# Two key batches of the cache moved into the feed-forward's inner rows, and the sample group's products gathered into fewer groups

## The chip, the cores and the metric

The kernel runs on one core of a Trainium2 chip. Its time is the device time of one execution in microseconds (us); less is better. The engines are PE (TensorE), DVE (VectorE), ACT (ScalarE), POOL (GpSimd) and SP (SyncE), which here issues the DMA transfers. Each engine works through its own list of instructions in order and waits on semaphores, so an instruction that waits also holds up all behind it on that engine.

## What is computed

One inference step of a decoder layer, for 256 prompt tokens and 8 sample tokens (one new token for each of 8 sequences, with 1024 cached positions each in 8 pages of 128):

```python
def trunk_layer(x, ...):
    x = x + 0.5 * swiglu_ffn(x, ffn1_norm, ffn1_w_in, ffn1_w_out)
    h = rmsnorm(x, mix_norm)
    u, q, k, v, qm = split(h @ w_in)                  # 1024 -> 256 + 3*512 + 256
    y_pool = pool_mixer(u, state_pool)
    q, k = rotary(rmsnorm(q)), rotary(rmsnorm(k))
    y_moba = moba_attention(q, concat(k_cache[pages], k), concat(v_cache[pages], v))
    y_mem = mem_attention(rmsnorm(qm), mk, mv)
    x = x + concat(y_pool, y_moba, y_mem) @ w_out
    return x + 0.5 * swiglu_ffn(x, ffn2_norm, ffn2_w_in, ffn2_w_out)
```

Everything is float32. A product of two float32 matrices is made of three products of rounded parts (`three`): high by high, high by low, low by high.

## The kernel before, in words

**Stages.** The first feed-forward (its inner rows, then its output product, called FFN1 out here, until 215.8 us), the mix stage (projections and all attention, until about 345 us), the output projection, and the second feed-forward.

**Weights** come through a ring of four raw buffers in units of 128x1024. SP loads a unit, ACT makes its high part (`w_hi`), DVE its low part (`w_lo`), PE uses both. FFN1 out has 22 units, numbers 48 to 69, of 24 matmuls each. The last two are taken together, bank by bank (`last_two`): PE waits for both low parts ahead of the first of its 48 matmuls.

**Key pages.** The cached keys of the eight sequences come in batches k0 to k7 of eight pages. DVE turns each batch by four STREAM_TRANSPOSE instructions of two pages each ("turn pairs", G 0 to G 31, counted in `k_turned8`), and then PE makes the batch's scores (K 0 to K 7, `key_logits`, which waits for that count). There are four slots of `kv`, an `early_slot` for k4 and a `late_slot` for values. Batches k0 to k3 are loaded in FFN1 and turned in FFN1 out; k4 to k7 are loaded and turned in the mix stage, k5 to k7 as slots come free (`free_wait`).

**The order of the mix stage** is written by hand. The projection has 16 steps r, each of four blocks P(r, tt, kk) of three 128x512 matmuls on PE. The table `EXTRA[r][i]` gives the tokens that every engine goes through ahead of block i of step r (i = 4: behind the step), and `TAIL` what follows the 16 steps. Each engine picks out the tokens that concern it, so the table sets the order on each engine. The tokens used below:

- PE: S r (sample tokens' product of step r, from the raw unit: a raw buffer is not loaded anew before its S is done), K b (key scores), V b (products with cached values), T (turns of q and k), HA h, HB h, PV h (prompt attention of head pair h: scores, turn of probabilities, product with values), MG (turn of a memory-key page; MG k waits for the copy of page k-1), A 1, A 4, A 5 (sums in the sample softmax), Y.
- ACT: W (high part of a unit), ET and ES (copies out of the projection's banks for prompt and samples; ET counts `t_evac`), HE (exponentials), HT, and the copies of even memory-key pages.
- DVE: WL (low part), G (turn pairs), NR, NQ, NV, NS, NG, ND (norms and rotary parts; NR 2 waits for ET 1), OWN, A 0, A 2, A 4 (sample softmax), HM (mask and maximum), HV (scaling of probabilities, which HB waits for), and the copies of odd memory-key pages.

S, K and V write narrow column ranges (8 or 32 columns of the array for each instruction, several ranges at once). In the table of before they stand mostly one by one between P blocks.

Of the kernel before, what the change touches and what calls it, by code (L numbers as in the profile page):

```python
# [15 lines left out]
P = 128  # L16
D = 1024
KT = D // P
DFF = 2816
HT = DFF // P  # L20
NS = 8
# [36 lines left out]
EARLY_PAIRS, AWAKE, AWAKE_2 = 16, 12, 3  # L58
# [12 lines left out]
HELD = (4, 5, 6, 7)  # L71

EARLY_SLOT, LATE_SLOT = KV_SLOTS, KV_SLOTS + 1
SLOT_OF = {("k", 0): 0, ("k", 1): 1, ("k", 2): 2, ("k", 3): 3, ("k", 4): EARLY_SLOT, ("k", 5): 0, ("k", 6): 1, ("k", 7): 2,
           ("v", 0): 3, ("v", 1): 0, ("v", 2): 1, ("v", 3): 2, ("v", 4): LATE_SLOT, ("mk", 0): 3, ("v", 5): 0, ("mv", 0): 1,
           ("v", 6): 2, ("v", 7): LATE_SLOT}
# [34 lines left out]
def layer(nc, a):  # L111

    ctx = ExitStack()
    with ctx:
# [96 lines left out]
        at[0] = region  # L211
        qp = over("qp", [P, 2, 512])
        at[0] = late_end
        early_slot = place("early_slot", [P, PAGES * 512], at=at[0])
        vp = over("vp", [P, 2, 512])
        up = over("up", [P, 2, 512])
        kT = over("kT", [P, 4, NP])
        prob_pair = over("prob_pair", [P, 2, 2, NP])
        kp = over("kp", [P, 2, 512])
        probT_pair = [probT_even, over("probT_odd", [P, 2 * NP])]  # L220
        q4 = over("q4", [P, P])
        k4 = over("k4", [P, P])
        v4 = over("v4", [P, P])
        u4 = over("u4", [P, P])
        qm_cols = place("qm_cols", [P, 2, NS, 32], at=at[0])
        qT = over("qT", [P, 4, NP])
        qmT = over("qmT", [P, 2, NP])
        mkT = over("mkT", [P, 2, NP])
        pm_cols = over("pm_cols", [P, 2, P])
        ys = over("ys", [P, KT, NS])  # L230
        stats = over("stats", [P, 80])
        m_stats = over("m_stats", [P, 4])
        joined = over("joined", [P, 3, P])
        same, repeat, quarter_of = joined[:, 0, :], joined[:, 1, :], joined[:, 2, :]
        own_y = over("own_y", [P, 2, 4, 4])
        v_cols = over("v_cols", [P, P])
        marks = over("marks", [P, 8])
        half_mark, two_mark = marks[:, 4:6], marks[:, 6:8]
        sq_one = over("sq_one", [P, 1, P])
# [6 lines left out]
        rm_pos = over("rm_pos", [P, 2 * CH])  # L246

# [9 lines left out]
        kv_loaded = [[sem(f"kv_loaded{i}_{h}") for h in range(2)] for i in range(KV_SLOTS + 2)]  # L257
# [59 lines left out]
        slots = [kv[:, i, :] for i in range(KV_SLOTS)] + [early_slot[:], late_slot[:]]  # L317
# [14 lines left out]
        def free_wait(eng, kind, b):  # L332

            if kind == "k" and b == 4:
                eng.wait_ge(w_used, U_WIN)
            elif kind == "k" and b > 4:
                eng.wait_ge(k_used, b - 4)
            elif kind == "v" and b < 5:
                eng.wait_ge(k_used, (4, 6, 7, 8, 8)[b])
            else:  # L340
                eng.wait_ge(v_used, {"mk": 1, "mv": 3}[kind] if kind != "v" else {5: 2, 6: 4, 7: 5}[b])
# [52 lines left out]
        def keys_of(u, t):  # L394
# [26 lines left out]
        }  # L421
        TAIL = ([("T", 4), ("NQ", 6), ("HV", 6), ("HV", 7), ("POOL", 0), ("MG", 4), ("HB", 6), ("HT", 6), ("HB", 7), ("HT", 7), ("MG", 5), ("NV", 6), ("ND", 5),
# [25 lines left out]
        def _(sp):  # L448
# [31 lines left out]
            def load_page(kind, b, t):  # L480

                if kind == "k":
                    if b in PAIRED:
                        pages[b, t] = page_of(b, t)
                    page = pages[b, t]
                elif b in PAIRED:
                    page = ((pairs[b, t // 2] >> 8) if t % 2 else (pairs[b, t // 2] & 255)).with_bounds(min_val=0, max_val=a["cache_v"].shape[1] - 1)
                else:
                    page = pages.pop((b, t))
                done = kv_loaded[SLOT_OF[kind, b]][t // 4]  # L490
                if kind == "k":
                    sp.dma_start(slots[SLOT_OF["k", b]][:, t * 512:(t + 1) * 512],
                                 a["cache_k"][0, ds(page, 1)].rearrange("o p h d -> p (o h d)")).then_inc(done, 16)
                else:
                    sp.dma_start(value_rows(b, t), a["cache_v"][0, ds(page, 1)].rearrange("o (b k) h d -> k (o b) (h d)", b=4)).then_inc(done, 16)
# [72 lines left out]
            for k in range(HT):  # L568
                load_unit(U_OUT1, k, 0, ffn_out[0][:, k:k + 1, :])
                if k >= HT - 2 * len(HELD):  # L570
                    for t in range(4):
                        at_ = HELD[(k - HT + 2 * len(HELD)) // 2], k % 2 * 4 + t
                        pages[at_] = page_of(*at_)
                if k == LATE_KEYS - 1:
                    sp.wait_ge(w_used, U_MEM + 4)
                if LATE_KEYS <= k < LATE_KEYS + PAGES:
                    load_page("k", 3, k - LATE_KEYS)
                    if (k - LATE_KEYS) % 2:
                        pair_pages(3, k - LATE_KEYS)
# [20 lines left out]
            load_batch("k", 4)  # L600
# [4 lines left out]
            load_batch("k", 5)  # L605
            load_projection(8)
            load_batch("k", 6)
            load_projection(9)
            load_batch("k", 7)
            load_projection(10)  # L610
            load_batch("v", 0)
            load_projection(11)
            load_projection(12)
            load_batch("v", 1)
            load_projection(13)
            load_projection(14)
            load_projection(15)
            load_batch("v", 2)
# [75 lines left out]
        def _(act):  # L694
# [196 lines left out]
            for what, k in steps():  # L891
# [16 lines left out]
                elif what == "T":  # L908
                    if k == 2:
                        act.wait_ge(k_used, 5)  # L910
# [97 lines left out]
        def _(vec):  # L1008
# [20 lines left out]
            def turn_pair(g):  # L1029

                kv_wait(vec, "k", g // 4, (g % 4 // 2,))
                vec.transpose(key_pair(g), key_pair(g)).then_inc(k_turned8, 1)  # L1032
# [269 lines left out]
            vec.wait_ge(const_set, 5)  # L1302
            ffn_out_loop(0, 0, 1)
# [4 lines left out]
            for n in range(16):  # L1308
                split(U_OUT[0] + 2 + 4 + n)
                if n < EARLY_PAIRS:  # L1310
                    turn_pair(n)
# [190 lines left out]
        def _(pe):  # L1502
# [149 lines left out]
            def key_logits(b):  # L1652
# [6 lines left out]
                pe.wait_ge(k_turned8, 4 * (b + 1))  # L1659
# [340 lines left out]
```

## Time and profile before

| | before |
|---|---|
| time, median of 3 runs | 560.54 us (560.49 to 561.45) |
| profiled execution: its span | 559.2 us |
| PE busy | 551.3 us, 99% of the span |
| DVE busy | 398.9 us, 71% |
| ACT busy | 269.2 us, 48% |
| granted TensorE clock | 1.000 |

The span runs from the first to the last instruction of the profiled execution; the median lies 1.3 us above it. Busy times of engines overlap; the time is set by the engine that others wait for.

### The profile page before, as it was taken

The numbers are of one execution on the slowest core, as the hardware profiler recorded it, in microseconds if no ns is written. First come the engines' busy times: TensorE is split into PE (matmuls) and PEld (weight loads), VectorE is DVE, ScalarE is ACT, GpSimd is POOL, SyncE is SP. The second block draws the span as 40 slices with busy tenths as digits, with TensorE's granted clock in tenths as the row PEclk, the third lists the DMA queues.
The fourth block names the chain that finished last, engine by engine and source line by source line (L and its number), as shares of the span: only waits on it lengthen the run. The fifth ranks groups of instructions, "written<-read, shape, count | busy, mean of one in ns | idle before, by whom it ended". The sixth has DMA issues, their size and how long they took to land.

```text
span 559.2 us, 13391 instructions
## 1 busy us (share of the span) xinstructions
PE 551.3 (99%) x5075; PEld 513.6 (92%) x5075; DVE 398.9 (71%) x715; ACT 269.2 (48%) x425; POOL 17.7 (3%) x24
## 2 busy tenths in 40 slices
PE   8999999999999999999999999999999999999997
PEld 8999999999899998666777679999999999999997
DVE  4687888885588877889946685689777777664444
ACT  5844464444543337344535785475444344433330
POOL 1000000000000003100000000140000000000000
PEclk9999999999999999999999999999999999999999
DMA  9799999784567664899999994566756666465523
GB/s 236 208 269 324 271 315 268 234 249 149 196 216 273 205 209 160 273 338 382 351 300 371 373 337 143 163 180 197 211 168 191 182 175 194 132 220 181 187 75 79
DMA packets 137481, 128.40 MB, mean 230 GB/s; under 512 B 10937, under 2 KB 108880, under 8 KB 137432
## 3 DMA queue, kind: packets, MB, share of 16 engines
q1 hardware_dynamic: 134703, 127.24, 72.8%
q10 hardware_dynamic: 2736, 0.61, 0.5%
q8 instruction: 26, 0.43, 0.3%
q14 instruction: 16, 0.12, 0.1%
HBM read 125.12 MB, written 2.83 MB: 229 GB/s over the span
## 4 chain that ended last, share of the span: by engine, by line
PE 85%; DVE 7%; DMA 3%; ACT 2%; issue 1%; SPq 0%; DVEq 0%; ACTq 0%
PE banks L1505 25%; PE banks L1506 25%; PE banks L1507 25%; PE banks L1665 3%; PE banks L1513 2%; DVE w_lo L1021 2%; PE banks L1939 1%; PE banks L1637 1%; DMA raw<-in_ffn_w_in 1%; PE banks L1890 1%; DMA x_rows<-in_x_sample 1%; DMA page_ids<-in_page_table 1%; PE banks L1866 1%; ACT x_hi L827 1%; DVE prob_pair L1448 1%
## 5 line engine op out<-in xcount | busy, mean ns | idle before, releaser
L701 ACT ACTIVATE w_hi<-raw 128x1024 fp32r<-128x1024 f32 x158 | 166.5, 1059 | 194.9 <-PE banks L1507 160.8
L1021 DVE TENSOR_TENSOR w_lo<-raw,w_hi 128x1024 fp32r<-128x1024 f32 x158 | 193.8, 1232 | 73.9 <-ACT w_hi L701 72.7
L1505 PE MATMUL banks<-x_hi,w_hi 128*128 128x264 f32 x752 | 214.1, 285 | 0.1
L1506 PE MATMUL banks<-x_lo,w_hi 128*128 128x264 f32 x752 | 213.0, 283 | 0.0
L1507 PE MATMUL banks<-x_hi,w_lo 128*128 128x264 f32 x752 | 213.0, 283 | 0.0
L1505 PEld LDWEIGHTS banks<-x_hi,w_hi 128*128 128x128 f32 x752 | 141.6, 188 | 0.7 <-issue 0.4
L1506 PEld LDWEIGHTS banks<-x_lo,w_hi 128*128 128x128 f32 x752 | 141.7, 188 | 0.0
L1507 PEld LDWEIGHTS banks<-x_hi,w_lo 128*128 128x128 f32 x752 | 141.0, 188 | 0.0
L1505 PE MATMUL banks<-h_hi,w_hi 128*128 (+1 forms) x352 | 100.2, 285 | 0.0
L1507 PE MATMUL banks<-h_hi,w_lo 128*128 (+1 forms) x352 | 100.2, 285 | 0.0
L1506 PE MATMUL banks<-h_lo,w_hi 128*128 (+1 forms) x352 | 100.0, 284 | 0.0
L1506 PEld LDWEIGHTS banks<-h_lo,w_hi 128*128 128x128 f32 x352 | 66.5, 189 | 0.0
L1505 PEld LDWEIGHTS banks<-h_hi,w_hi 128*128 128x128 f32 x352 | 66.2, 188 | 0.3 <-ACT mem_kv L879 0.3
L1507 PEld LDWEIGHTS banks<-h_hi,w_lo 128*128 128x128 f32 x352 | 66.3, 188 | 0.0
L1065 DVE TENSOR_TENSOR h_tmp<-banks,rstd 128x264 f32<-128x264 f32 x44 | 18.9, 429 | 22.7 <-PE banks L1507 22.7
L1032 DVE STREAM_TRANSPOSE kv<-kv 128x1024 f32<-128x1024 f32 x28 | 33.9, 1228 | 0.0
L1505 PE MATMUL banks<-w_hi,x_hi 128*128 128x512 f32 x64 | 28.0, 438 | 0.3 <-ACT qp L794 0.3
L726 ACT ACTIVATE sg<-sg 128x264 f32<-128x264 f32 x44 | 18.3, 415 | 18.2 <-DVE sg L1060 18.2
L1507 PE MATMUL banks<-w_hi,x_lo 128*128 128x512 f32 x64 | 25.3, 395 | 0.0
L1506 PE MATMUL banks<-w_lo,x_hi 128*128 128x512 f32 x64 | 25.2, 394 | 0.0
L1074 DVE TENSOR_TENSOR h_lo<-h_tmp,h_hi 128x264 f32 (+1 forms) x44 | 19.1, 434 | 3.6
L1070 DVE TENSOR_TENSOR h_tmp<-sg,h_tmp 128x264 f32<-128x264 f32 x44 | 19.0, 433 | 3.3 <-ACT sg L726 2.0
(287 smaller groups left out, 501.7 us busy)
## 6 DMA issues: line engine op xcount, KB each, us to landing
raw<-in_ffn_w_in SPq DMA_DIRECT2D x86, 512.0 KB, 4.8
raw<-in_ffn_w_out SPq DMA_DIRECT2D x44, 512.0 KB, 3.4
kv<-in_cache_k SPq DMA_DIRECT2D x56, 256.0 KB, 4.8
kv<-in_cache_v SPq DMA_DIRECT2D x48, 256.0 KB, 6.3
raw<-in_w_in SPq DMA_DIRECT2D x12, 512.0 KB, 5.2
late_slot<-in_cache_v SPq DMA_DIRECT2D x16, 256.0 KB, 4.6
raw<-in_w_out SPq DMA_DIRECT2D x8, 512.0 KB, 7.5
raw<-in_mem_w_kv SPq DMA_DIRECT2D x4, 512.0 KB, 4.0
```

Of the source, the lines that this page charges most:

```text
L701: act.activation(w_hi[:, n % RING, :], raw[:, n % RING, :], ACT.Copy).then_inc(hi_ready, 1)
L726: act.activation(sg[:, s, :], sg[:, s, :], ACT.Silu).then_inc(silu_ready, 1)
L1021: vec.tensor_tensor(w_lo[:, n % RING, :], raw[:, n % RING, :], w_hi[:, n % RING, :].bitcast(F32), ALU.subtract).then_inc(lo_ready, 1)
L1032: vec.transpose(key_pair(g), key_pair(g)).then_inc(k_turned8, 1)
L1065: vec.tensor_tensor(h_tmp[:, s, :], bank[b0 + 2 * s + 1][:, 0:N], rstd[:], ALU.mult).then_inc(gu_free, 1)
L1070: vec.tensor_tensor(h_tmp[:, s, :], sg[:, s, :], h_tmp[:, s, :], ALU.mult).then_inc(hm_ready, 1)
L1074: vec.tensor_tensor(h_lo[:, ds(c, 1), :].rearrange("p a n -> p (a n)"), h_tmp[:, s, :], h_hi[:, ds(c, 1), :].rearrange("p a n -> p (a n)") ...
L1505: pe.matmul(out, lhs[0], rhs[0], start=start, stop=False)
L1506: pe.matmul(out, lhs[0], rhs[1], start=False, stop=False)
L1507: return pe.matmul(out, lhs[1], rhs[0], start=False, stop=stop)
L1513: return pe.transpose(out, in_, ident[0:k, 0:k])
L1665: mm = pe.matmul(bank[LG_BANK][32 * hp:32 * hp + 32, half * NP:(half + 1) * NP], q_cols[:, c0:c0 + 32], keys[:, 4 * hp + c], start=(b4 == ...
```

## The change

Batches k4 and k5 get two hidden slots of their own, which lie over the inner rows `h_hi` and `h_lo` of the first feed-forward. A unit of FFN1 out uses up one inner row, and as soon as enough rows are used (`w_used`), SP loads a page of each batch over them. So 24 turn pairs, G 0 to G 23, are done before and in FFN1 out, and k6 and k7 take the slots of k0 and k1 in the mix stage. Values take other slots. Small tiles get other places in memory. In the table, K 0 to K 3 stand together, S 4 to S 7 with K 4 and K 5, K 6 and K 7 with S 8 to S 11, V 0 with V 1, V 3 with S 12 to S 15, and the sample softmax and the prompt attention begin about a step earlier. The diff, cut to its core (of the table a line only):

```diff
-HELD = (4, 5, 6, 7)
+HELD = (6, 7)
+HIDDEN = (4, 5)
+LEAD_PAIRS = (0, 1, 2)
+EARLY_PAIRS = ((3,), (4,), (5, 16), (6,), (7, 20), (8, 17), (9,), (10, 21), (11,), (12, 18), (13,), (14, 22), (15,), (19,), (23,), ())
...
+        slot_bytes, half_bytes = 4 * PAGES * 512, 4 * HT * N
+        hidden_slots = [place(f"hidden_slot{i}", [P, PAGES * 512], at=region + i * half_bytes) for i in range(2)]
...
-            elif kind == "k" and b > 4:
-                eng.wait_ge(k_used, b - 4)
+            if kind == "k":
+                eng.wait_ge(k_used, b - 5)
             elif kind == "v" and b < 5:
-                eng.wait_ge(k_used, (4, 6, 7, 8, 8)[b])
+                eng.wait_ge(k_used, (3, 4, 7, 8, 8)[b])
...
             for k in range(HT):
                 load_unit(U_OUT1, k, 0, ffn_out[0][:, k:k + 1, :])
+                if k >= 6 and k % 2 == 0:
+                    t = k // 2 - 3
+                    sp.wait_ge(w_used, U_OUT1 + 2 * t + 2)
+                    for b in HIDDEN:
+                        pages[b, t] = page_of(b, t)
+                        load_page("k", b, t)
...
-            load_batch("k", 4)
+            sp.wait_ge(w_used, U_WIN)
...
-            load_batch("k", 5)
+            load_batch("k", 6)
+            load_batch("k", 7)
             load_projection(8)
-            load_batch("k", 6)
             load_projection(9)
-            load_batch("k", 7)
...
+            for g in LEAD_PAIRS:
+                turn_pair(g)
...
                 split(U_OUT[0] + 2 + 4 + n)
-                if n < EARLY_PAIRS:
-                    turn_pair(n)
+                for g in EARLY_PAIRS[n]:
+                    turn_pair(g)
...
-                pe.wait_ge(k_turned8, 4 * (b + 1))
+                pe.wait_ge(k_turned8, 4 * (b + 1) if b in HELD else 4 * HELD[0])
...
-            6: {0: [("NG", 3)], 1: [("G", 28)], 2: [("G", 29)], 3: [("WL", 9), ("G", 30)], 4: [("S", 8)]},
+            6: {0: [("NG", 3)], 1: [("G", 28)], 2: [("G", 29)], 3: [("WL", 9), ("G", 30)], 4: [("G", 31)]},
```

On DVE, in steps 3 and 4, the list of before has the turn pairs of k4 (early_slot) and of k5 (kv) on both sides of NR 2, whose first instructions are the four `rot<-qp`:

```order
L1021 TENSOR_TENSOR w_lo<-raw,w_hi 128x1024
L1032 STREAM_TRANSPOSE early_slot<-early_slot 128x1024 x4
L1032 STREAM_TRANSPOSE kv<-kv 128x1024 x2
L1164 TENSOR_TENSOR rot<-qp,rope_q 128x128 x4
L1172 TENSOR_TENSOR qp<-rot 128x16x8
L1173 TENSOR_TENSOR qp<-rot 128x16x8
L1032 STREAM_TRANSPOSE kv<-kv 128x1024 x2
L1129 TENSOR_REDUCE ss_h<-sq_h 128x16
```

The same place in the changed list:

```order
L1037 TENSOR_TENSOR w_lo<-raw,w_hi 128x1024
L1183 TENSOR_TENSOR rot<-qp,rope_q 128x128 x4
L1191 TENSOR_TENSOR qp<-rot 128x16x8
L1192 TENSOR_TENSOR qp<-rot 128x16x8
L1148 TENSOR_REDUCE ss_h<-sq_h 128x16
```

Six pairs ahead of NR 2 and two behind its rotary part have gone to FFN1 out; the other eight, of k6 and k7, stay behind NR 2.

On PE, around the first head pair's scores (HA 0, `kT,qT`), before had V 0, a P block, HA 0, S 13 and V 1 in this order, then three P blocks (nine rows like the last, left out), then HB 0:

```order
L1939 MATMUL banks<-kv,p_cols 8x128 x32
L1505 MATMUL banks<-w_hi,x_hi 128x512
L1506 MATMUL banks<-w_lo,x_hi 128x512
L1507 MATMUL banks<-w_hi,x_lo 128x512
L1866 MATMUL banks<-kT,qT 128x128 x2
L1866 MATMUL banks<-kT,qT 128x256 x2
L1637 MATMUL banks<-raw,xs 8x128 x8
L1939 MATMUL banks<-kv,p_cols 8x128 x32
L1505 MATMUL banks<-w_hi,x_hi 128x512
```

After, V 0 and V 1 stand ahead of HA 0, and behind it come three P blocks and HB 0 (`prob_pair`):

```order
L1960 MATMUL banks<-kv,p_cols 8x128 x64
L1887 MATMUL banks<-kT,qT 128x128 x2
L1887 MATMUL banks<-kT,qT 128x256 x2
L1526 MATMUL banks<-w_hi,x_hi 128x512
L1527 MATMUL banks<-w_lo,x_hi 128x512
L1528 MATMUL banks<-w_hi,x_lo 128x512
```

S 13 and V 1 no longer stand between HA 0 and HB 0; S 14 and V 3 leave the place between HA 1 and HB 2, and V 4 with a memory-key page that between HA 2 and HB 4.

On PE, at the end of step 7, the changed list has K 6 and K 7 (32 instructions) and S 8 to S 11 (32) next to each other:

```order
L1528 MATMUL banks<-w_hi,x_lo 128x512
L1686 MATMUL banks<-kv,q_cols 32x256 x32
L1658 MATMUL banks<-raw,xs 8x128 x32
L1526 MATMUL banks<-w_hi,x_hi 128x512
L1527 MATMUL banks<-w_lo,x_hi 128x512
L1528 MATMUL banks<-w_hi,x_lo 128x512
L1847 MATMUL banks<-own_by_half,joined 128x8
```

In the list of before K 7 stands a step later, behind S 10, and the six products stand at five places; from NR 2's release to K 6 the changed list has 16 P blocks, T 0 and T 1.

## Rows read from the trace of the kernel before

**Rows 1.** The page's first part: busy time, share of the span, instructions.

```profile
PE 551.3 (99%) x5075; PEld 513.6 (92%) x5075; DVE 398.9 (71%) x715; ACT 269.2 (48%) x425; POOL 17.7 (3%) x24
```

**Rows 2.** The list of waits, PE: total us, times, longest us.

```profile
PE banks L1513 <- DVE prob_pair L1448: 0.7, 1, 0.7
PE banks L1513 <- ACT kv L722: 0.6, 1, 0.6
PE banks L1505 <- ACT qp L794: 0.3, 1, 0.3
```

**Rows 3.** Timeline of DVE in FFN1 out: start, duration, instruction, idle before it.

```profile
190.75 1.22 DVE L1021 TENSOR_TENSOR w_lo<-raw,w_hi 128x1024 fp32r<-128x1024 f32 x1 [0.53 <-ACT w_hi L701]
193.69 1.23 DVE L1021 TENSOR_TENSOR w_lo<-raw,w_hi 128x1024 fp32r<-128x1024 f32 x1 [0.56 <-ACT w_hi L701]
```

**Rows 4.** Timeline of SP: loads of units 68 and 69, four page numbers read between them.

```profile
193.87 0.33 SPq L456 DMA_DIRECT2D raw<-in_ffn_w_out  x1
196.42 0.33 SPq L456 DMA_DIRECT2D raw<-in_ffn_w_out  x1
```

**Rows 5.** DMA issues of FFN out units: count, KB each, median us to landing.

```profile
raw<-in_ffn_w_out SPq DMA_DIRECT2D x44, 512.0 KB, 3.4
```

**Rows 6.** Timeline of PE around S 0 to S 3.

```profile
220.21 0.39 PE L1507 MATMUL banks<-w_hi,x_lo 128*128 128x512 f32 x1
220.53 1.93 PE L1637 MATMUL banks<-raw,xs 128*8 128x128 f32 x64
222.39 0.50 PE L1505 MATMUL banks<-w_hi,x_hi 128*128 128x512 f32 x1
222.73 0.39 PE L1506 MATMUL banks<-w_lo,x_hi 128*128 128x512 f32 x1
```

**Rows 7.** Timeline of PE: K 4 and T 0.

```profile
242.62 1.93 PE L1665 MATMUL banks<-early_slot,q_cols 128*32 128x256 f32 x32
...
246.68 0.60 PE L1513 MATMUL banks<-ident,qp 128*128 128x128 f32 x4
```

**Rows 8.** Timeline of DVE: the start of NR 2, and G 30 and G 31.

```profile
241.86 0.85 DVE L1164 TENSOR_TENSOR rot<-qp,rope_q 128x128 f32<-128x128 f32 x4
...
260.75 2.36 DVE L1032 STREAM_TRANSPOSE kv<-kv 128x1024 f32<-128x1024 f32 x2
```

**Rows 9.** Busy times from NR 2's start to the end of G 31: window, length, engines, clock, DMA share, GB/s.

```profile
241.70:263.11 21.41, 21.41 (x193) 14.25 (x192) 19.81 (x37) 8.75 (x13) 0.00 (x0) 1.00 1.02 373
```

**Rows 10.** Timeline of DVE: starts of OWN 0 and A 0, and A 4's last.

```profile
264.14 0.28 DVE L1201 TENSOR_TENSOR rot<-q,k 128x128 f32<-128x128 f32 x1
...
266.48 0.69 DVE L1375 TENSOR_REDUCE stats<-banks 128x8 f32<-128x512 f32 x1
...
278.34 0.60 DVE L1410 TENSOR_SCALAR p_own<-ones,stats 128x128 f32<-128x128 f32 x2
```

**Rows 11.** Timeline of PE: S 13, V 1, P, HB 0; then S 14 and P.

```profile
284.67 0.62 PE L1637 MATMUL banks<-raw,xs 128*8 128x128 f32 x16
285.11 1.93 PE L1939 MATMUL banks<-kv,p_cols 128*8 128x128 f32 x64
286.97 0.50 PE L1505 MATMUL banks<-w_hi,x_hi 128*128 128x512 f32 x1
...
289.16 1.15 PE L1513 MATMUL banks<-ident,prob_pair 128*128 128x128 f32 x6
...
294.47 0.62 PE L1637 MATMUL banks<-raw,xs 128*8 128x128 f32 x16
295.02 0.50 PE L1505 MATMUL banks<-w_hi,x_hi 128*128 128x512 f32 x1
```

**Rows 12.** Timeline of DVE: HV 0, two scalings.

```profile
288.50 0.55 DVE L1448 TENSOR_SCALAR prob_pair<-prob_pair,rc 128x128 f32<-128x128 f32 x2
```

**Rows 13.** Busy times of line L1706's matmuls (all alike) at the program's start.

```profile
1.00:3.80 2.80, 2.80 (x13) 2.80 (x14) 1.00 0.85 201
3.80:5.30 1.50, 1.48 (x13) 1.28 (x12) 1.00 0.63 158
```

More of the change, by code:

```diff
@@ L57 @@
 ACT_PAGES = (0, 2, 4, 6)
-EARLY_PAIRS, AWAKE, AWAKE_2 = 16, 12, 3
+AWAKE, AWAKE_2 = 12, 3
 UNITS = 12
@@ L70 @@
 PAIRED = (0, 1, 2, 3)
-HELD = (4, 5, 6, 7)
[L73 to L76, printed above, removed]
+HELD = (6, 7)
+HIDDEN = (4, 5)
+LEAD_PAIRS = (0, 1, 2)
+EARLY_PAIRS = ((3,), (4,), (5, 16), (6,), (7, 20), (8, 17), (9,), (10, 21), (11,), (12, 18), (13,), (14, 22), (15,), (19,), (23,), ())
+LATE_SLOT = KV_SLOTS + len(HIDDEN)
+SLOT_OF = {("k", 0): 0, ("k", 1): 1, ("k", 2): 2, ("k", 3): 3, ("k", 4): KV_SLOTS, ("k", 5): KV_SLOTS + 1, ("k", 6): 0, ("k", 7): 1,
+           ("v", 0): 2, ("v", 1): 3, ("v", 2): 0, ("v", 3): 1, ("v", 4): LATE_SLOT, ("mk", 0): 2, ("v", 5): 3, ("mv", 0): 0,
+           ("v", 6): 1, ("v", 7): LATE_SLOT}
 BY_POOL = ()
@@ L210, in layer @@
         x_wide = over("x_wide", [P, 3, P])
-        at[0] = region
+        slot_bytes, half_bytes = 4 * PAGES * 512, 4 * HT * N
+        hidden_slots = [place(f"hidden_slot{i}", [P, PAGES * 512], at=region + i * half_bytes) for i in range(2)]
+        at[0] = region + slot_bytes
         qp = over("qp", [P, 2, 512])
[L213 to L220, printed above, removed]
+        joined = over("joined", [P, 3, P])
         q4 = over("q4", [P, P])
         k4 = over("k4", [P, P])
+        assert at[0] <= region + half_bytes
+        at[0] = region + slot_bytes
+        qmT = over("qmT", [P, 2, NP])
         v4 = over("v4", [P, P])
         u4 = over("u4", [P, P])
-        qm_cols = place("qm_cols", [P, 2, NS, 32], at=at[0])
-        qT = over("qT", [P, 4, NP])
-        qmT = over("qmT", [P, 2, NP])
+        v_cols = over("v_cols", [P, P])
+        ys = over("ys", [P, KT, NS])
+        own_y = over("own_y", [P, 2, 4, 4])
+        at[0] = region + half_bytes + slot_bytes
         mkT = over("mkT", [P, 2, NP])
+        probT_pair = [probT_even, over("probT_odd", [P, 2 * NP])]
         pm_cols = over("pm_cols", [P, 2, P])
-        ys = over("ys", [P, KT, NS])
+        sq_one = over("sq_one", [P, 1, P])
         stats = over("stats", [P, 80])
         m_stats = over("m_stats", [P, 4])
[L233 to L236, printed above, removed]
         marks = over("marks", [P, 8])
-        half_mark, two_mark = marks[:, 4:6], marks[:, 6:8]
-        sq_one = over("sq_one", [P, 1, P])
         own4 = over("own4", [P, 4])
@@ L246, in layer @@
         rm_pos = over("rm_pos", [P, 2 * CH])
+        same, repeat, quarter_of = joined[:, 0, :], joined[:, 1, :], joined[:, 2, :]
+        half_mark, two_mark = marks[:, 4:6], marks[:, 6:8]
+        at[0] = region + slot_bytes // 2
+        assert at[0] >= late_end
+        kp = over("kp", [P, 2, 512])
+        vp = over("vp", [P, 2, 512])
+        at[0] = region + half_bytes
+        qm_cols = place("qm_cols", [P, 2, NS, 32], at=at[0])
+        qT = over("qT", [P, 4, NP])
+        up = over("up", [P, 2, 512])
+        kT = over("kT", [P, 4, NP])
+        prob_pair = over("prob_pair", [P, 2, 2, NP])
         banks = ctx.enter_context(nc.psum_tensor("banks", [P, 8, 512], F32))
@@ L256, in layer @@
         raw_loaded = [sem(f"raw_loaded{i}") for i in range(RING)]
-        kv_loaded = [[sem(f"kv_loaded{i}_{h}") for h in range(2)] for i in range(KV_SLOTS + 2)]
+        kv_loaded = [[sem(f"kv_loaded{i}_{h}") for h in range(2)] for i in range(LATE_SLOT + 1)]
+        hidden_loaded = [sem(f"hidden_loaded{q}") for q in range(PAGES // 2)]
         pool_loaded = kv_loaded
@@ L315, in layer @@
         w_in, w_mix, w_mem = cols_view(a["w_in"], KT), cols_view(a["w_out"], KT), cols_view(a["mem_w_kv"], KT)
-        slots = [kv[:, i, :] for i in range(KV_SLOTS)] + [early_slot[:], late_slot[:]]
+        slots = [kv[:, i, :] for i in range(KV_SLOTS)] + [slot[:] for slot in hidden_slots] + [late_slot[:]]
         def kv_wait(eng, kind, b, parts=(0, 1)):
@@ L332, in free_wait @@
         def free_wait(eng, kind, b):
-            if kind == "k" and b == 4:
-                eng.wait_ge(w_used, U_WIN)
-            elif kind == "k" and b > 4:
-                eng.wait_ge(k_used, b - 4)
+            if kind == "k":
+                eng.wait_ge(k_used, b - 5)
             elif kind == "v" and b < 5:
-                eng.wait_ge(k_used, (4, 6, 7, 8, 8)[b])
+                eng.wait_ge(k_used, (3, 4, 7, 8, 8)[b])
             else:
@@ L401, in layer @@
             2: {1: [("QT", 0), ("WL", 3)], 4: [("QT", 2), ("SS", 0), ("WL", 4)]},
[19 rows of a table removed]
-        }
-        TAIL = ([("T", 4), ("NQ", 6), ("HV", 6), ("HV", 7), ("POOL", 0), ("MG", 4), ("HB", 6), ("HT", 6), ("HB", 7), ("HT", 7), ("MG", 5), ("NV", 6), ("ND", 5),
[1 row of a table removed]
[21 rows of a table added]
+        }
+        TAIL = ([("T", 4), ("NQ", 6), ("POOL", 0), ("MG", 4), ("MG", 5), ("NV", 6), ("ND", 5),
[1 row of a table added]
                  ("QT", 1), ("V", 6), ("HV", 8), ("HV", 9), ("HA", 5), ("HM", 10), ("HM", 11), ("HY", 1), ("HB", 8), ("HT", 8),
@@ L489, in load_page @@
                     page = pages.pop((b, t))
-                done = kv_loaded[SLOT_OF[kind, b]][t // 4]
+                done = hidden_loaded[t // 2] if kind == "k" and b in HIDDEN else kv_loaded[SLOT_OF[kind, b]][t // 4]
                 if kind == "k":
@@ L612, in _ @@
             load_projection(11)
+            load_batch("v", 1)
             load_projection(12)
-            load_batch("v", 1)
             load_projection(13)
+            load_batch("v", 2)
             load_projection(14)
             load_projection(15)
-            load_batch("v", 2)
             load_batch("v", 3)
@@ L908, in _ @@
                 elif what == "T":
-                    if k == 2:
-                        act.wait_ge(k_used, 5)
+                    if k == 0:
+                        act.wait_ge(k_used, 6)
                     turned([k])
@@ L1029, in turn_pair @@
             def turn_pair(g):
-                kv_wait(vec, "k", g // 4, (g % 4 // 2,))
+                if g // 4 in HIDDEN:
+                    vec.wait_ge(hidden_loaded[g % 4], 16 * 2 * len(HIDDEN))
+                else:
+                    kv_wait(vec, "k", g // 4, (g % 4 // 2,))
                 vec.transpose(key_pair(g), key_pair(g)).then_inc(k_turned8, 1)
```

40 rows, old and new, of tables (EXTRA, TAIL) are left out of this document.

## Prediction

> **What bounds the kernel now.** I read the page's first part, then the list of waits, then the timelines. PE is busy for 551.3 of 559.2 us [rows 1], and its list of waits has, apart from the start, only pieces below 1 us [rows 2]. So PE sets the time, nearly every other engine's work is covered, and the order in the mix stage leaves little slack: HB 0 starts on PE at 289.16, and DVE ends its scaling HV 0 at 288.50 + 0.55 = 289.05 [rows 11, 12]. From this follow the two questions. What does the change take off PE? And where does it take PE's cover away from a chain on DVE or ACT, so that PE now waits?
>
> **What it takes off PE.** No product is dropped; only visits to narrow groups are joined. What a visit costs beyond its work: the step into the group is 220.53 - 220.21 = 0.32 us and the first step behind it 222.73 - 222.39 = 0.34 [rows 6], where P matmuls in a run are (2.19 - 0.11) / 9 = 0.23 apart (three blocks from 286.97 to 289.16, the first step 0.11 long) [rows 11]. Besides, S 14 alone takes 295.02 - 294.47 = 0.55 and S 13, with V 1 right behind it, 285.11 - 284.67 = 0.44 [rows 11]. So a visit costs 0.09 + 0.11 + 0.11 = 0.31. Counted in the two tables, eight full visits go (K 2, K 4, K 5, one of S 8 to S 11's four, and so on) and three partial ones (V 0, S 14, S 15) of some 0.17 each: **-3.0** (bounds -3.4, -2.0). PE's wait for the copy of `qp` goes too, as K 4 and K 5 now stand in front of that block: **-0.3** [rows 2].
>
> **The end of FFN1 out.** DVE has 0.53 us idle in each unit of 2.94 us beside a split and a turn pair [rows 3]. Over 16 units that is 8.5 us, and five more pairs cost 5 x 1.18 = 5.9 [rows 8], three going ahead. DVE fits. SP is closer: with four page numbers between two loads it issues one every 2.55 us [rows 4], so a number takes (2.55 - 0.37) / 4 = 0.55. Now it waits until 14 units are used, at about 215.8 - 8 x 2.94 = 192.3, and must then issue two times six numbers, four more, four pages (some 0.5 each, as a load takes 0.33 and its register work) and two loads before unit 69's: 16 x 0.55 + 2.0 + 0.8 = 11.6, to 203.9 instead of 196.42. It lands 3.4 later [rows 5]; with the low part 1.22 [rows 3] and the high part taken as long, it is ready at 209.7 at best, each hand-over adding some 0.1 to 0.2. PE wants it for units 68 and 69 together, at 215.8 - 2 x 2.94 = 209.9. A page that lands late or a later wait of SP makes it about 1 us late; the residual and S 0 follow. I take **+1.0** (0 to 2.2).
>
> **K 7 waits for G 31.** In before DVE has turn pairs to do until just ahead of NR 2, which starts at 241.86 [rows 8]. The change takes these six away, but NR 2 can't start earlier, because it waits for ET 1, and ET 1 for a P block that now stands behind K 4 and K 5 as well. DVE then stands idle there, and behind NR 2 lie eight pairs still. From NR 2 to the end of G 31 before took 21.41 us, with DVE busy for 19.81 [rows 9]. Without two pairs it takes 21.4 - 2 x 1.18 = 19.05. Add about 1.0 from the end of the P block to NR 2 (ACT's copy and two hand-overs, an estimate, 0.7 to 1.5): G 31 ends 20.1 after that block. PE has in the same time 16 P blocks of 0.70, two T of about 0.4, and K 6 (1.93 with its tail, 1.75 to 1.86 without [rows 7]): 11.2 + 0.8 + 1.8 = 13.8. K 7 so waits 20.1 - 13.8 = **+6.3** (5.3 to 7.0). In before the same end of G 31, at 263.11, was just ahead of K 7, which stood a step (2.8 us) and three visits later. Nothing covers it: S 8 to S 11, the sample softmax and all P blocks are behind K 7 on PE.
>
> **A 5 waits for the sample softmax.** From the start of A 0 to the end of `p_own` DVE took 278.34 + 0.60 - 266.48 = 12.5 us in before. OWN 0 and a norm's part, 266.48 - 264.14 = 2.3, stood ahead of A 0 [rows 10] and now stand in that chain: 14.8. PE has from K 7 to A 5 the products S 8 to S 11 (1.75), 13 P blocks (9.1) and small sums (some 0.8): 11.7. **+2.9** (1.5 to 3.4).
>
> **HB 0, HB 2 and HB 4 lose their cover.** From HA 0's end to HB 0 are 289.16 - 284.67 = 4.5 us of PE work: S 13 and V 1 (286.97 - 284.67 = 2.30) and three P blocks (2.19) [rows 11]. DVE's and ACT's chain in that time ends 0.11 before HB 0 [rows 12]. Only the three P blocks are left: **+2.2**. The same chain lies between HA 1 and HB 2, where S 14 (0.55) and V 3 (286.97 - 285.11 = 1.86, like V 1) go: 2.4 less a slack of a few tenths, **+2.2** (1.7 to 2.4 each). Between HA 2 and HB 4 no split stands in DVE's chain, so it is 4.4 - 1.2 = 3.2 against three P blocks and Y 0 (2.6): 0.6, and HB 5, whose scaling ends about 1.2 later, another 0.9 behind 0.3 of PE work: **+1.4** (0.8 to 1.8).
>
> **Memory-key pages.** The three pages of MG 4 to MG 6 now stand back to back, and MG 2 close behind HA 3. Each waits for the copy of the page before, which on DVE or ACT queues behind the masks and exponentials of a head pair. The one such wait before is 0.6 [rows 2]. For MG 2 the copy stands behind two masks; bounds 0 and 2.2 (what HB loses to the same queue), nearer to two such waits: **+1.2**. MG 5 and MG 6 against HB 6's 0.7 that goes [rows 2], with small waits elsewhere: **+0.6** (0 to 1.2).
>
> **Sum.** -3.0 - 0.3 + 1.0 + 6.3 + 2.9 + 2.2 + 2.2 + 1.4 + 1.2 + 0.6 = +14.5 us. Against the profiled span, 559.2 + 14.5 = 573.7; the median lies 1.3 above its span, so 575.0. What lies behind (the rest of attention, the output projection, FFN2) is PE's own work and moves back by the same amount. Transfers for values gain time by it, so they aren't a new limit.
>
> **Rivals.** *The clock falls in the wait.* Six us without a matmul is longer than any wait in this trace behind the start. What the trace shows of a cold start: of the same matmul 13 take 2.80 us at first and then 1.48 us [rows 13], the rates of 1.2 and 2.4 GHz, while the granted clock reads 1.00 in both, so the step shows in the spacing alone. If PE came back at the low rate behind K 7's wait for as long as at the start (some 2.8 us of work), K 7 and S 8 to S 11 (3.6 us of PE work) would lose about 1.4, and up to 2.5 with a second such fall: 576.4 to 577.5. No row of before has a wait that decides it. The Trainium skill, "TensorE: Matmul & The Clock Gate", Part 1, says that TensorE falls to 1.2 GHz behind an idle window and comes back only when it has been busy again; by that rule the time is the higher one, 576.4.
>
> *The turning fits and only the joining counts: faster.* What decides is when G 31 ends. If NR 2 is released about 6 us earlier than I hold, or DVE gets through the eight pairs in the idle time of 19.81 to 21.41, K 7 doesn't wait; the softmax and the HB chains would then also have to run ahead. The single mechanism is the visits: 560.5 - 3.3 = 557.2. Against it: NR 2's release hangs on PE's own order, and DVE's 19 us are busy to over nine tenths [rows 9].
>
> *Half of the waits hide each other.* A wait of 6.3 at K 7 lets ACT, DVE and the loads run ahead. If A 5 and two of the HB chains so find their inputs ready, the sum is 14.5 - 2.9 - 4.4 = 7.2: 567.7. Against it: each of these chains begins with a PE product behind the wait.
>
> *The hidden pages come late.* Then DVE, which turns two pairs in six of the units, holds up the splits in FFN1 out, and PE waits there: a late page of 3 us costs up to 3 more, 578. Against it: a page has some four units to land.
>
> **How the numbers follow.** The sum's chance is 0.48; the fallen clock 0.24; half the waits 0.16; late pages 0.05; faster 0.04; no change, if joining and waits cancel, 0.03. Predicted is the likeliest, 575.0. The sum's low bounds give -3.4 + 0 + 5.3 + 1.5 + 1.7 + 1.7 + 0.8 + 0 + 0 - 0.3 = +7.3, 567.8; the high ones -2.0 + 2.2 + 7.0 + 3.4 + 2.4 + 2.4 + 1.8 + 2.2 + 1.2 - 0.3 = +20.3, 580.8. Not all terms go one way at once, but the clock and the rivals use up the difference: 567.5 to 580.5. Faster by over 0.2% (about what this measurement can tell from none): 0.04; within: 0.03; slower: 0.93.
>
> **What would show it.** In the changed profile PE should wait some 6 us for DVE's turn pairs at K 7, 2 to 3 us for `p_own` at A 5, about 2 us each for `prob_pair` at HB 0 and HB 2, and at the page turns; DVE should stand idle for some 10 us before NR 2. If K 7's matmuls start with G 31 long done, the main term is wrong. If the narrow groups aren't shorter by 3 us in all, the joining is. If matmuls behind K 7's wait are twice as far apart as later, the clock is the rival that holds.

## The result and the profile after

The changed kernel takes 582.12 us (median of 4 runs, 580.80 to 583.30) against 561.00 for the kernel before; ratio 1.037 (95% interval 1.035 to 1.039). It is slower by 21 us, 3.7%. Medians here leave out one slow execution of experiment 2 (690.31 us, mean granted clock 0.749) and one of experiment 9 (570.43 us). The direction and the places were forecast, the size was not: 575.0 with a range to 580.5.

The profiled execution is the fastest of the four (580.8 us). Its span is 579.0 us, 19.8 more than before's, and PE's own work hardly grew. The page's head and first part:

```profile
span 579.0 us, 13392 instructions
...
PE 553.8 (96%) x5075; PEld 517.7 (89%) x5075; DVE 399.0 (69%) x715; ACT 269.6 (47%) x425; POOL 17.7 (3%) x24
```

Against [rows 1] PE is busy 2.5 us longer although no product was added, and the rest of the 19.8 us is waiting. The list of waits of PE in the changed kernel (total us, times, longest us):

```profile
PE banks L1686 <- DVE kv L1051: 6.2, 1, 6.2
PE banks L1534 <- DVE prob_pair L1469: 5.4, 4, 2.1
PE banks L1534 <- DVE p_own L1431: 3.0, 1, 3.0
PE banks L1534 <- DVE kv L1043: 2.9, 2, 2.0
PE banks L1960 <- issue: 1.5, 1, 1.5
...
PE banks L1534 <- ACT kv L738: 0.8, 1, 0.8
```

L1686 are the key scores (K 7), L1469 the scaling of probabilities (HB 0, 2, 4, 5), L1431 is `p_own` (A 5), L1043 and L738 are the copies of memory-key pages (MG 2, 5, 6), and L1960 is a pause inside V 1, for which the profile shows no releaser. In [rows 2] the same list held 1.8 us in the mix stage, counting 0.2 at A 5; now it holds 20.0, counting 0.2 at S 0.

The timeline of DVE shows the idle time ahead of NR 2 that was expected, then NR 2's first rows:

```profile
233.64 1.22 DVE L1037 TENSOR_TENSOR w_lo<-raw,w_hi 128x1024 fp32r<-128x1024 f32 x1
245.32 0.90 DVE L1183 TENSOR_TENSOR rot<-qp,rope_q 128x128 f32<-128x128 f32 x4 [10.46 <-ACT qp L810]
```

And the timeline of PE shows what came with the wait at K 7:

```profile
256.53 1.93 PE L1686 MATMUL banks<-kv,q_cols 128*32 128x256 f32 x32
...
264.70 3.64 PE L1686 MATMUL banks<-kv,q_cols 128*32 128x256 f32 x32 [6.24 <-DVE kv L1051]
268.12 2.19 PE L1658 MATMUL banks<-raw,xs 128*8 128x128 f32 x64
271.04 0.38 PE L1847 MATMUL banks<-own_by_half,joined 128*128 128x8 f32 x2
```

K 6 and K 7 are 32 matmuls each, of the same shape. K 6 takes 1.93 us with its tail, as K 4 did in [rows 7], and K 7 takes 3.64. Busy times by window (length, PE, PEld, DVE, ACT, POOL, granted clock, DMA share, GB/s) say why:

```profile
262.00:264.00 2.00, 0.00 (x0) 0.00 (x0) 2.00 (x3) 0.00 (x0) 0.00 (x0) 0.50 0.02 9
266.00:267.00 1.00, 1.00 (x16) 0.54 (x12) 0.00 (x0) 0.00 (x0) 0.00 (x0) 0.50 0.00 0
269.00:270.00 1.00, 1.00 (x44) 0.92 (x40) 0.97 (x4) 0.00 (x0) 0.00 (x0) 1.00 0.00 0
341.00:342.00 1.00, 1.00 (x7) 0.49 (x4) 0.34 (x3) 0.98 (x2) 0.00 (x0) 0.50 1.04 383
```

The granted clock fell to 0.50 (1.2 GHz) while PE waited at K 7, stayed there through K 7's own time, and was 1.00 (2.4 GHz) again from S 9 on. A second such stretch lies at 341 us, behind the page turns MG 5 and MG 6, two waits of 0.8 and 0.9 us. The window from 241.70 in [rows 9], and every other of before, had 1.00.

**Where the 19.8 us are.** The mix stage begins 0.27 us later, and the first product of the output projection (`x_hi,w_hi`) 19.8 us later. The two lines of before, then those of the changed kernel:

```profile
215.81 0.40 PE L1505 MATMUL banks<-w_hi,x_hi 128*128 128x512 f32 x1
338.11 0.39 PE L1505 MATMUL banks<-x_hi,w_hi 128*128 128x264 f32 x1
...
216.08 0.40 PE L1526 MATMUL banks<-w_hi,x_hi 128*128 128x512 f32 x1
357.88 0.39 PE L1526 MATMUL banks<-x_hi,w_hi 128*128 128x264 f32 x1
```

Between the two lie 18.2 us more of waits (20.0 - 1.8). Work at the low clock adds 3.6: K 7 1.7 (3.42 to the next product, against 1.73 in a joined group), S 8 0.3, HA 4 0.9 and the pooling product 0.7. What remains, 19.5 - 18.2 - 3.6 = -2.3, is put down to joining the narrow products. It is a remainder and not a measurement, and experiments 8 and 11 bear on it.

### The profile page after: what moved, and what is told of

It reads as the page before. It is cut to its first block, busy times and chain, and to the rows that moved or that the text cites. A ratio compares the mean times of both kernels' runs of the same rounds, so it can differ in the third digit from the quotient of the medians.

```text
span 579.0 us, 13392 instructions
## 1 busy us (share of the span) xinstructions
PE 553.8 (96%) x5075; PEld 517.7 (89%) x5075; DVE 399.0 (69%) x715; ACT 269.6 (47%) x425; POOL 17.7 (3%) x24
## 4 chain that ended last, share of the span: by engine, by line
PE 78%; DVE 11%; ACT 3%; DMA 3%; issue 2%; SPq 1%; DVEq 0%; POOL 0%; ACTq 0%; POOLq 0%
PE banks L1526 21%; PE banks L1527 21%; PE banks L1528 21%; PE banks L1960 3%; PE banks L1534 3%; DVE w_lo L1037 2%; PE banks L1686 2%; DVE kv L1051 2%; DMA raw<-in_ffn_w_in 1%; PE banks L1887 1%; PE banks L1658 1%; PE banks L1911 1%; PE banks L1727 1%; SPq L488 1%; ACT w_hi L717 1%
## 5 line engine op out<-in xcount | busy, mean ns | idle before, releaser
L1051 DVE STREAM_TRANSPOSE kv<-kv 128x1024 f32<-128x1024 f32 x24 | 29.0, 1227 | 0.0
```

## The experiments

The theory behind the prediction: the time lies in the order table, in chains on DVE and ACT that lost the PE work over them. The clock was a rival of its own. Each time below is a median, each list, timeline or window is of one profiled execution, and before, run again beside them, had medians of 561.05 to 561.81.

**1. PE kept busy in K 7's wait** (on the changed kernel):

```diff
 elif what == "K":
+    if k == 7:
+        for _ in range(54):
+            pe.matmul(bank[1][:, 0:P], ones[:], ones[:], start=True, stop=True)
     key_logits(k)
```

> The changed kernel with 54 idle matmuls (128x128, ones by ones, into a bank that nothing uses there) on PE just ahead of the wait of K 7, so that PE is not idle in it. Theory (a wait lets the clock fall, and that costs by itself): the wait as such stays, K 7 starts within 0.3 us of where it did, but its 32 matmuls take 1.75 us instead of 3.42 and S 8 takes 0.44 instead of 0.71, so the time is 2.0 us below the changed kernel's. Rival (K 7 is slow for another reason, such as contention, and the low clock beside it costs nothing): K 7 still takes over 3 us and the time is the changed kernel's within 0.5 us.

588.48 us, slower. The edit was too large: the profile records each of these float32 matmuls as two, 108 in 12.32 us, so PE was busy for twice the wait. K 7 behind them took 1.75 us to the next product. The low clock came back later, at A 5, HB 0 and the page turns.

**2. The same with 27.**

> As the run with 54 idle matmuls ahead of K 7's wait, with 27: each such matmul was recorded as two of 0.114 us, so 27 fill 6.2 us, which is the wait. Theory (the low clock behind the wait costs by itself): K 7 begins within 0.3 us of where it did in the changed kernel, its matmuls take 1.75 us instead of 3.42, and the time is about 2 us below the changed kernel's, as far as the clock does not fall at a later wait instead; where it does, up to 1.5 us of this is given back. Rival (the low clock is no cost of its own): the time is the changed kernel's within 0.5 us.

580.62 us, 1.5 below the changed kernel. The timeline of PE:

```profile
260.05 6.29 PE L1829 MATMUL banks<-ones 128*128 128x128 f32 x54
266.38 1.93 PE L1686 MATMUL banks<-kv,q_cols 128*32 128x256 f32 x32
268.13 1.93 PE L1658 MATMUL banks<-raw,xs 128*8 128x128 f32 x64
```

and two later windows:

```profile
284.30:287.70 3.40, 3.40 (x14) 2.80 (x12) 0.64 (x3) 1.22 (x3) 0.00 (x0) 0.50 1.07 393
298.00:301.30 3.30, 3.30 (x12) 2.07 (x12) 0.00 (x0) 1.45 (x3) 0.00 (x0) 0.50 1.08 367
```

The wait is as long as before and K 7 is back at 1.75, so the low clock is a cost of its own, 2.0 us there with S 8. The clock then fell behind A 5's and HB 0's waits instead, at full PE work, which cost 1.6 us (7.95 from A 5 to HA 0, against 6.36 in experiment 6) and 1.5 us (6.73 from HB 0 to HA 1, against 5.23 in the changed kernel), and it did not fall at the page turns. The profiled execution so took 580.62 us against the changed kernel's 580.80: the gain shows in K 7's rows, hardly in the time.

**3. PE kept busy in four waits** (27 matmuls at K 7, and in the same way 13 at A 5, and 9 each at HB 0 and HB 2).

> The changed kernel with idle matmuls that fill the waits at K 7 (27), A 5 (13), HB 0 and HB 2 (9 each), so that PE is not idle in the four longest waits ahead of the page turns. Theory (each fall of the clock behind a wait costs by itself): no low clock between 250 and 310 us, at most the one behind the page turns near 340; about 2.5 us below the run with 27, so 578.5, with less spread between executions than the changed kernel's 2.5 us. Rival: the clock falls anyway, and the time stays at 581 or above.

577.56 us. In the windows of the profile the clock is now whole up to the page turns; it falls at 326 us, behind MG 2's wait of 2.0 us:

```profile
256.00:270.00 14.00, 13.96 (x191) 10.93 (x189) 12.75 (x24) 3.68 (x5) 0.00 (x0) 1.00 0.54 190
270.00:320.00 50.00, 48.27 (x598) 39.21 (x602) 27.91 (x92) 22.07 (x54) 0.00 (x0) 1.00 0.80 262
320.00:335.00 15.00, 12.84 (x174) 10.04 (x164) 6.59 (x19) 7.36 (x17) 0.53 (x1) 0.89 1.05 369
```

Nothing of DVE's or ACT's work was moved, and 4.6 us went (582.1 - 577.6). V 1's pause is absent here too, so up to 1.5 of the 4.6 may be that. The executions still spread over 2.8 us, so that part of the expectation fell.

**4. The turn pairs of k6 ahead of NR 2.**

```diff
-4: {0: [("NQ", 2)], 1: [("NR", 2)], ...
+4: {0: [("NQ", 2), ("G", 24), ("G", 25), ("G", 26), ("G", 27)], 1: [("NR", 2)], ...
```

> The changed kernel with the four turn pairs of batch k6 (G 24 to G 27) moved ahead of NR 2 on DVE, into the 10.5 us in which DVE stood idle there. Theory (K 7 waits because DVE's turn pairs stand behind NR 2): the wait at K 7 falls from 6.2 us by the 4.7 us of four pairs, to about 1.5, the clock does not fall there, and the time is 4.7 + 2.0 = 6.7 us below the changed kernel's. Rival (the pages of k7 land late, or NR 2 itself is late): the wait stays above 5 us and the time moves by less than 1 us.

578.03 us, 4.1 below. K 7's row:

```profile
261.45 3.37 PE L1686 MATMUL banks<-kv,q_cols 128*32 128x256 f32 x32 [2.11 <-DVE kv L1051]
```

The wait fell by 4.1 of the 4.7 us expected, so its cause is as stated. The time fell short of the 6.7 expected, since even behind 2.1 us of waiting the clock was low, and the 2.0 us for it stayed.

**5. V behind HA.**

```diff
-("V", 0), ("V", 1), ("HA", 0), ("HM", 0), ("HM", 1), ("HE", 0), ("HE", 1)
+("HA", 0), ("HM", 0), ("HM", 1), ("HE", 0), ("HE", 1), ("V", 0), ("V", 1)
```

and in the same way V 2 behind HA 1, V 3 with S 12 to S 15 behind HA 2, V 4 behind HA 3.

> The changed kernel with the products with cached values (V 0 and V 1, V 2, V 3 with S 12 to S 15, V 4) put behind the scores HA 0, HA 1, HA 2, HA 3 instead of ahead of them; nothing else is moved. Theory (the scaling chain lost its cover): the waits at HB 0, HB 2, HB 4 and HB 5 (2.1, 2.1, 0.6, 0.7 us) and the one at MG 2 (2.0) go, each covered by 1.9 to 3.6 us of V and S; about 7 us below the changed kernel's. Rival (the chain is late because of DVE or ACT queues, and moves with the products): the waits stay within 0.5 us of their length. The pause of 1.5 us inside V 1 should stay if it comes from V 0 and V 1 standing together.

572.45 us, 9.7 below. From the list of waits:

```profile
PE banks L1534 <- DVE kv L1043: 1.1, 2, 0.9
...
PE banks L1534 <- DVE prob_pair L1469: 0.2, 1, 0.2
```

5.2 of the 5.4 us of waits at the four HB and 1.8 at MG 2 are gone, with no work moved on DVE or ACT. The pause in V 1 (1.5) went too, though V 0 and V 1 still stand together, so their standing together does not make it by itself. That is 8.5 us. The profiled execution, the slowest of the four, gained 7.7, and its clock was at 0.50 in three stretches: at K 7, A 5 and the page turns.

**6. OWN 0 and NV 4 ahead of A 0.**

```diff
-7: {2: [("WL", 10)], ... ("A", 0), ("ET", 3), ("NQ", 4), ("W", 11)]}
-8: {0: [("OWN", 0)], 1: [("OWN", 1)], 2: [("NV", 4), ("ND", 4)], ...
+7: {2: [("WL", 10), ("OWN", 0)], ... ("ET", 3), ("NQ", 4), ("NV", 4), ("A", 0), ("W", 11)]}
+8: {1: [("OWN", 1)], 2: [("ND", 4)], ...
```

> The changed kernel with OWN 0 and NV 4 ahead of A 0 on DVE, where DVE has time for them while PE makes K 7 and S 8 to S 11. Theory (A 5 waits because 2.3 us of other work entered the softmax chain): the wait at A 5 falls from 3.0 us to about 1.3, the time by 1.7 us. Rival (the chain is bound by ACT or by the splits in it): the wait stays above 2.5 us.

582.07 us, and the wait at A 5 stays:

```profile
283.50 0.33 PE L1534 MATMUL banks<-ident,v 128*128 128x128 f32 x1 [3.01 <-DVE p_own L1431]
```

The theory of that wait fell. DVE now idles for 1.2 and 1.3 us where these instructions stood, waiting for the product of `own_by_half` and for A 1 on PE, which stand behind P blocks there. The timeline of DVE in the changed kernel shows what stands between A 2 and A 4:

```profile
275.51 0.69 DVE L1422 TENSOR_TENSOR rows<-banks,stats 128x512 f32<-128x512 f32 x1
276.12 2.35 DVE L1037 TENSOR_TENSOR w_lo<-raw,w_hi 128x1024 fp32r<-128x1024 f32 x2
278.39 0.24 DVE L1166 RECIPROCAL rs_h<-sd_h 128x16 f32<-128x16 f32 x1
...
283.06 0.60 DVE L1431 TENSOR_SCALAR p_own<-ones,stats 128x128 f32<-128x128 f32 x2
```

These are two splits and the keys' norm; before had one split and the same norm there.

**7. One of the two splits (WL 11) ahead of A 0.**

```diff
-("S", 11), ("A", 0), ("ET", 3), ("NQ", 4), ("W", 11)]}
+("S", 11), ("W", 11), ("WL", 11), ("A", 0), ("ET", 3), ("NQ", 4)]}
...
-9: {0: [("WL", 11), ("ES", 2)], ...
+9: {0: [("ES", 2)], ...
```

> The changed kernel with the split WL 11 on DVE ahead of A 0 instead of behind A 2, into DVE's idle time behind G 31. The earlier reason for A 5's wait (OWN 0 and NV 4 in the chain) fell, since it stayed at 3.0 us without them. New theory: between A 2 and A 4 DVE now has two splits (2.35 us) and the norm of the keys, where before had one split, while PE has one P block and S 12 less; without one split the wait at A 5 falls by 1.1 to 1.2 us, to 1.8, and the time by as much. Rival (A 4 waits for ACT's exponentials): the wait stays at 3.0.

The wait, in the timeline of PE:

```profile
284.63 0.33 PE L1534 MATMUL banks<-ident,v 128*128 128x128 f32 x1 [1.85 <-DVE p_own L1431]
```

1.2 us less, as expected. The median is 579.82 us, but the executions run from 577.3 to 582.9 with mean granted clocks from 0.993 to 0.985, so the 1.2 us can't be read from the time.

**8. Three edits at once** (4, 5 and 6 on the changed kernel).

> The changed kernel with three edits at once: the turn pairs of k6 ahead of NR 2, the products V behind the scores HA, and OWN 0 and NV 4 on DVE ahead of A 0. Theory (the waits are separate and add up): 4.1 us, 9.7 us and 1.7 us below the changed kernel's 582.1, so 566.6 (564 to 569), with waits of about 2 us at K 7, 1.3 at A 5, 1 at MG 2 and 1.9 at MG 5 and MG 6 left. Rival (a wait that goes turns up again at the next chain): over 570.

566.49 us (564.6 to 569.3). The time is as stated, but not all of its parts: the wait at A 5 stays at 3.0 us, where 1.3 was expected, and one of 0.8 for a batch of values is new. Without A 5's 1.7 us the stated sum is 568.3, which is within the spread, so the closeness is in part luck. In the profiled execution the clock stayed at 1.00, K 7 included, behind the same wait as in 4:

```profile
261.12 1.93 PE L1686 MATMUL banks<-kv,q_cols 128*32 128x256 f32 x32 [2.11 <-DVE kv L1051]
```

So here the remainder, put down to joining, can be taken without the low clock. The mix stage, from its first product to that of the output projection, takes 125.1 us, 2.8 more than in before, with 8.3 us of waits, 6.5 more: -3.7, not -2.3. Part of the difference is that a product behind a wait is slower than the wait says: the six matmuls of HB 0 take 0.96 us to the next step behind their wait in the changed kernel, and 0.57 here, without one. The rest, and what V behind HA adds to it, was not tried apart.

**9. And the tail's order of before** (4, 5 and 6 with NV 4 put back, WL 11 ahead of A 0, and HB 6, HB 7, PV 3 and MG 4 to MG 6 as in before).

> The changed kernel with the turn pairs of k6 ahead of NR 2, V behind HA, WL 11 ahead of A 0, and the tail's order of before for HB 6, HB 7, PV 3 and MG 4 to MG 6. Theory (the waits at MG 5 and MG 6 come from the three page turns standing together): they fall from 0.8 and 0.9 us to under 0.3 each, and with A 5's 1.2 the time is about 2.7 us below the 566.5 of the three edits, so 563.8. Rival (DVE's masks and scalings are late there anyway): HB 6 and HB 7 wait instead, and only A 5's 1.2 is won.

567.11 us (9 runs, 561.98 to 569.93), where 563.8 was expected: no gain over 8. From the list of waits:

```profile
PE banks L1686 <- DVE kv L1051: 2.1, 1, 2.1
PE banks L1960 <- DMA kv<-in_cache_v: 2.0, 1, 2.0
PE banks L1534 <- DVE p_own L1431: 1.9, 1, 1.9
...
PE banks L1534 <- DVE kv L1043: 0.2, 1, 0.2
```

The page turns' waits are gone as expected and A 5's is smaller, but PE now waits 2.0 us for a batch of values. In 8 that wait was 0.8. As PE gets earlier, loads come due: S 8 to S 11 stand behind K 7, and SP waits for S 8 ahead of the raw load of step 12 (10.5 us in the changed kernel, in the list of waits of SP), with all values from v2 on queued behind it. That this makes the 2.0 us was not tried apart.

**10. The hidden slots alone**: the changed kernel with the order table of before, without G 16 to G 23.

> The hidden slots alone: the changed kernel's loads, slots and early turn pairs with the order table of before (only its tokens G 16 to G 23 left out, as these pairs are done in FFN1 out). Theory (the loss lies in the order table, not in the loads over the inner rows): the time is that of before within 1.5 us, FFN1 out ends 0.3 us later, and no wait above 1 us appears on PE. Rival (loads and turns in FFN1 out, or the other slots of the values, cost what was lost): 3 us or more above before.

561.83 us, ratio 1.0014 (1.0004 to 1.0025). Loads over the inner rows, early turns, the other slots and places in memory cost 0.1% together. All but 0.8 of the 21 us comes with the order table.

**11. The hidden slots with some joins**: number 10, with K 0 to K 3 together, S 4 to S 7 with K 4 and K 5, S 8 to S 11 with K 6 and K 7 at the end of step 8, and the turn pairs of k6 ahead of NR 2. V, HA, HB, A 5 and the tail stand as in before.

```diff
+8: {0: [("OWN", 0)], 2: [("NV", 4), ("ND", 4)],
+    4: [("S", 8), ("S", 9), ("S", 10), ("S", 11), ("K", 6), ("K", 7), ("A", 0), ("OWN", 1)]},
```

> The hidden slots with the order table of before, into which only joins of S and K are taken that leave every chain its cover: K 0 to K 3 together, S 4 to S 7 with K 4 and K 5, and S 8 to S 11 with K 6 and K 7 at the end of step 8, the turn pairs of k6 ahead of NR 2; V, HA, HB and all behind stay as in before. Theory (joining saves 0.25 to 0.31 us for each visit where no cover is lost): seven visits fewer and no wait for qp, about 2 us below the hidden slots with the old table, so 559.8 us, 0.2% below before. Rival (each join costs a wait on a chain, or the raw buffers come back late since S 8 stands two steps later): no gain, 561.5 us or more.

559.51 us, ratio 0.9965 (0.9954 to 0.9976): faster than both kernels. The page's head and PE's longest waits behind the start:

```profile
span 557.8 us, 13392 instructions
...
PE banks L1531 <- DVE prob_pair L1466: 0.7, 1, 0.7
PE banks L1531 <- ACT kv L735: 0.7, 1, 0.7
```

2.3 us under number 10, and no wait above 0.2 us was added. Seven visits are joined and the wait of 0.3 for `qp` goes, so a visit gives 0.29, near the prediction's 0.31, where no chain loses its cover.

## Why the prediction was wrong

The direction, the places and all but one of the waits were right; the sum was too small by 5.3 us against the profiled execution (19.8 - 14.5). Term by term:

| term | forecast | measured |
|---|---|---|
| joining narrow products | -3.0 | -2.3 (remainder; -3.7 in experiment 8) |
| wait for `qp` goes | -0.3 | -0.3 |
| end of FFN1 out, with S 0 | +1.0 | +0.3, and 0.2 at S 0 |
| K 7 waits for G 31 | +6.3 | +6.2 |
| A 5 | +2.9 | +2.8 (3.0 - 0.2) |
| HB 0, HB 2 | +4.4 | +4.2 |
| HB 4, HB 5 | +1.4 | +1.2 |
| MG 2 | +1.2 | +1.4 (2.0, less 0.6 at MG 1 in before) |
| MG 5, MG 6, less HB 6 | +0.6 | +1.0 (1.7 - 0.7) |
| low clock | 0 (a rival: 1.4 to 2.5) | +3.6 |
| pause in V 1 | 0 | +1.5 |

**The step that failed is the sum**, which priced PE's work behind every wait at the full clock and kept the low clock as a rival at 0.24. Measured, that clock cost 3.6 us in the profiled execution, and the pause in V 1, a term the sum did not have, 1.5. Experiments 1 and 2 show in K 7's rows that the low clock is a cost of its own, and 3 that filling four waits, without moving any other work, takes 4.6 us off (up to 1.5 of it the pause). In the median it weighs more than in the profiled execution: the other three executions took 1.0 to 2.5 us longer at mean granted clocks of 0.988 and 0.982, against 0.991. The rival counted two falls of 2.8 us of work at most; there were two in the profiled execution, of 4.0 and 3.4 us of work, and the mean clocks suggest more or longer ones in the others.

The Trainium skill, "TensorE: Matmul & The Clock Gate", Part 1, says that TensorE falls to 1.2 GHz when it has been idle, and rises only when it has been busy again. The granted clock of 0.50 at K 7 and the return to 1.00 in S 8 agree. It also fell behind 2.1 us of waiting (4), and at 340 us behind two waits below 1 us.

**A 5 was right in size by accident.** Its wait was forecast from OWN 0 and NV 4 in the chain; experiment 6 takes these out and nothing changes. The wait comes from a second split ahead of A 4 (experiment 7, 1.2 of the 3.0 us) and, for the rest, from less PE work between A 1 and A 5: 7.96 us in the changed kernel, 9.66 in before. That part is read from the timelines, not tried. The forecast's own terms, 14.8 - 11.7, give 3.1; its 2.9 holds only less the 0.2 that A 5 waited in before, which it doesn't state.

**The pause in V 1** was not foreseen, and its cause stays open. A DMA of instructions lies in that time (the DMA view of 288.6 to 291.2 us):

```profile
q8 instruction: 1, 0.02, 2.5%
```

It turned up in 2 of the 7 profiled kernels with this PE order around V 1 (in the changed kernel and in 4, there 1.3 us), so the order does not settle it. Nor does that DMA: one lies in the time of V 0 and V 1 in experiments 1, 6 and 8 too, without a pause.

Of the rivals, the fallen clock held in its mechanism; its price, 1.4 to 2.5 us, was too small. Half the waits hiding each other did not: 6.2 us of waiting at K 7 made no later chain shorter. The pages in FFN1 out came in time but for three waits of 0.5 to 0.7 us on DVE, for which PE's list has no wait. The end of FFN1 out was read rightly: unit 69's load was issued at 204.31 (203.9 in the forecast), its low part was done at 209.99, and PE's step into that unit took 0.3 us longer.

## What to carry to other kernels

Before joining small products on the bounding engine, ask for each what chain on another engine ran under it: here a joined visit gave some 0.3 us, and one that had covered a chain cost 2. Price a new wait on TensorE with what follows it, as the clock may be low behind it; here that was a fifth of the loss. And take a rearrangement apart: the hidden slots cost 0.1%, part of the joins was a gain of 2.3 us, and the rest of the table lost far more.

## What the runs showed of the hardware

A fall of the clock is not settled by the length of the wait: behind the same 2.11 us at K 7 its 32 matmuls took 3.37 us in one kernel (4) and 1.93 in another (8). And matmuls put in as filler must be counted in the profile first: a float32 matmul of 128x128 is recorded as two, of 0.114 us each.
